# Last of sixteen experts added by a one-hot product instead of a scatter, with the other experts' sums reloaded beside it

## What is computed

```python
def expert_choice_ffn(h, w_router, w1, w3, w2):      # h: (B, L, D)
    cap = CAPACITY_FACTOR * L // N_EXPERTS           # 64 latent, 16 context tokens per expert
    aff = softmax(h @ w_router)
    gate, idx = lax.top_k(swapaxes(aff, 1, 2), cap)  # each expert chooses its tokens
    xs = h[idx]
    ye = (silu(xs @ w1) * (xs @ w3)) @ w2 * gate
    return zeros((L, D)).at[idx].add(ye)
...
x = x + g2 * expert_choice_ffn(h2, ...)
```

## Time and profile before

| | of the profiled execution |
|---|---|
| time, span | 3056.43 us, 3054.6 us |
| mean granted TensorE clock | 0.965 |
| PE busy | 2809.3 us (92%) |
| VectorE, ScalarE, GpSimd busy | 1882.3, 1501.3, 360.1 us |
| bytes moved by DMA | 595.31 MB |
| DMA rate while the experts run (page's slices) | 371 to 376 GB/s, most at 374 |
| cast of a 1 MB chunk, ScalarE | 1912 ns |
| low part of a chunk, VectorE | 2284 ns |
| load of 512 KB of w_in, issue to landing | 6.1 us (median of 72) |

### The profile page before, as it was taken

How to read it: one execution, slowest core, us unless ns; L and a number is a source line. 1 busy time by engine, 2 the same in 40 slices (tenths; PEclk the granted TensorE clock), 3 DMA queues, 4 the chain that set the end, 5 groups by cost and what they waited for, 6 DMA issues and landing times.

```text
span 3054.6 us, 40745 instructions
## 1 busy us (share of the span) xinstructions
PE 2809.3 (92%) x16674; PEld 2202.1 (72%) x16674; DVE 1882.3 (62%) x1929; ACT 1501.3 (49%) x1941; POOL 360.1 (12%) x233
## 2 busy tenths in 40 slices
PE   6999997999997999999879999989999599999996
PEld 5988876888875666666579777778889456666664
DVE  2166566652337888888633666658323578888884
ACT  4245454202127777777542455441122467777773
POOL 0411010000011101111113111100000211111110
PEclk8999999999998999999989999999999799999998
DMA  7132321221268999999822233122213399999995
GB/s 238 58 100 77 91 90 64 63 83 49 70 222 299 371 372 376 374 375 375 291 80 70 77 104 104 59 70 70 64 61 118 145 307 375 375 372 374 372 376 188
DMA packets 373482, 595.31 MB, mean 195 GB/s; under 512 B 12976, under 2 KB 164656, under 8 KB 373040
## 3 DMA queue, kind: packets, MB, share of 16 engines
q1 hardware_dynamic: 360208, 546.42, 51.0%
q0 software_dynamic: 13088, 46.28, 5.2%
HBM read 566.97 MB, written 25.69 MB: 194 GB/s over the span
## 4 chain that ended last, share of the span: by engine, by line
PE 70%; DMA 13%; DVE 7%; ACT 5%; issue 3%; SPq 1%; POOL 0%; DVEq 0%; POOLq 0%; ACTq 0%
PE ps L1270 17%; PE ps L1272 17%; PE ps L1271 17%; DMA m_raw<-in_w 9%; PE ps L1536 9%; DVE m_lo L1207 2%; PE ps L1461 2%; PE ps L1494 2%; DMA raw<-in_w_ada 1%; PE ps L1314 1%; ACT probs L520 1%; DVE stats L1020 1%; PE ps L1483 1%; DMA xg<-h_rows,token_of_slot 1%; SPq L314 1%
## 5 line engine op out<-in xcount | busy, mean ns | idle before, releaser
L798 ACT CAST m_hi<-m_raw 128x2048 fp32r<-128x2048 f32 x384 | 733.1, 1912 | 283.0 <-DMA m_raw<-in_w 264.4
L1207 DVE TENSOR_TENSOR m_lo<-m_raw,m_hi 128x2048 fp32r<-128x2048 f32 x384 | 861.5, 2284 | 14.3 <-PE ps L1272 13.2
L1270 PE MATMUL ps<-h_hi,w_hi 128*128 128x384 f32 (+2 forms) x1408 | 442.6, 314 | 17.1 <-DVE h_lo L943 9.4
L1272 PE MATMUL ps<-h_hi,w_lo 128*128 128x384 f32 (+2 forms) x1408 | 436.6, 310 | 0.0
L1271 PE MATMUL ps<-h_lo,w_hi 128*128 128x384 f32 (+2 forms) x1408 | 436.4, 310 | 0.0
L1270 PE MATMUL ps<-m_hi,xs_hi 128*80 128x512 f32 x1024 | 406.9, 397 | 3.4 <-DVE xs_lo L1224 3.4
L1271 PE MATMUL ps<-m_lo,xs_hi 128*80 128x512 f32 x1024 | 404.3, 395 | 0.0
L1272 PE MATMUL ps<-m_hi,xs_lo 128*80 128x512 f32 x1024 | 404.2, 395 | 0.0
L870 DVE TENSOR_TENSOR w_lo<-raw,w_hi 128x2048 fp32r<-128x2048 f32 x68 | 157.9, 2321 | 300.6 <-ACT w_hi L563 290.4
L563 ACT CAST w_hi<-raw 128x2048 fp32r<-128x2048 f32 x46 | 87.6, 1906 | 486.7 <-DMA raw<-in_w_gate 314.7
L1270 PE MATMUL ps<-w_hi,h_hi 128*128 128x256 f32 x960 | 284.4, 296 | 3.1 <-ACT pool_branch L647 1.8
(11 more groups left out here) (252 smaller groups left out, 4191.9 us busy)
## 6 DMA issues: line engine op xcount, KB each, us to landing
m_raw<-in_w SPq DMA_DIRECT2D x384, 1024.0 KB, 10.3
raw<-in_w_in SPq DMA_DIRECT2D x72, 512.0 KB, 6.1
raw<-in_w_ada SPq DMA_DIRECT2D x64, 512.0 KB, 4.7
raw<-in_w_gate SPq DMA_DIRECT2D x48, 512.0 KB, 6.7
ada_in_a<-in_w_ada SPq DMA_DIRECT2D x10, 1024.0 KB, 11.9
raw<-in_w_proj_a SPq DMA_DIRECT2D x16, 512.0 KB, 4.6
raw<-in_w_out SPq DMA_DIRECT2D x16, 512.0 KB, 6.0
moe_rows<-zeros POOLq DMA_DIRECT2D x10, 512.0 KB, 7.5
```

Source lines behind the costliest of these rows:

```text
L798: nc.scalar.copy(m_hi[:, g % HIS], m_raw[:, g % RAWS]).then_inc(s["m_high"], 1)
L1207: nc.vector.tensor_tensor(m_lo[:, g % LOS], m_raw[:, g % RAWS], m_hi[:, g % HIS].bitcast(F32), ALU.subtract).then_inc(s["msplit"], 1)
L1270: pe.matmul(out, wh, xh, start=first, stop=False, skip_group_check=True)
L1272: return pe.matmul(out, wl, xh, start=False, stop=last, skip_group_check=True)
```

## The change

The last expert is no longer scattered. Its result is split into `yh` and `yl` in SBUF (ScalarE and VectorE, one half of the channels at a time). A constant table with the token numbers 0 to 639 is loaded to 80 partitions (`places`), and VectorE compares it with each slot's token (`st[:, 62:63]`, a new copy at the routing), which gives the one-hot matrix `place` [80 slots, 640 tokens]. A product of `yh` and `yl` with `place` adds the rows at their tokens' columns, already transposed.

GpSimd loads `moe_rows`, which now holds the sums of the other 15 experts, as soon as expert 14's scatter has landed, beside the last expert's weights. `acc` becomes five tensors at places that are free then: two in slot 1 of `raw`, two behind `m_lo`, one in the value buffer. Because of the first two, SyncE's queue holds back layer 1's second load (slot 1) until all of TensorE's jobs are done.

TensorE's end is now 13 jobs. Jobs 0 to 4 transpose blocks 0 to 4 of `acc`, two after chunk 9 and three after chunk 10 of the last expert. Jobs 5 to 12 come after chunk 11, one for each block: a one-hot product for blocks 0 to 4, which VectorE adds to `x` in a second update; for blocks 5 to 7 the transposes are written as products with the identity and the one-hot product is added to them inside PSUM, with one update. The bank pairs are now 0, 2 and 6. The norm's sums move to banks 4 and 5. The split of the next layer's slot 0 comes after the last update on VectorE, that of slot 1 in the middle of the casts, as it does in layer 0.

```diff
+LAST_BANKS = (0, 2, 6)
+NTURN = 5
...
-        acc = sb("moe_tok", [P, TT, D], r_ring + 73728)
+        places = sb("token_numbers", [SLOTS, TOK], r_m)
+        place = sb("slot_of_token", [SLOTS, TOK], r_ring, F32R)
+        yh = sb("ye_hi", [SLOTS, D], r_ring + 4096, F32R)
+        yl = sb("ye_lo", [SLOTS, D], r_ring + 8192, F32R)
...
+        acc = [sb(f"moe_tok{t}", [P, D], at) for t, at in enumerate((r_raw + 8192, r_t2 + 32768, r_t2 + 36864, r_raw + 12288, r_v + 1280))]
...
@@ SyncE @@
                 for n, c0 in enumerate((POOL0, CONVB0, CONVA0)):
                     for u in range(2):
+                        if l and (n, u) == (0, 1):
+                            sp.wait_ge(s["acc_ps"], (NTURN + KT) * l)
                         wide(u, in_v[l, c0 // CW + u])
@@ GpSimd @@
                     pool.wait_ge(s["xs_ps"], seen("xs_ps"))
-                    if e < EXPERTS - 1:
-                        gather(e + 1)
+                    if e == EXPERTS - 1:
+                        pool.dma_start(places[:], places_in.partition_broadcast(SLOTS)).then_inc(s["places_in"], 16)
+                        break
+                    gather(e + 1)
...
-                    pool.dma_start(acc[:, t], moe_rows[t * P:(t + 1) * P, :]).then_inc(s["acc_in"], 16)
+                    pool.dma_start(acc[t][:], moe_rows[t * P:(t + 1) * P, :]).then_inc(s["acc_in"], 16)
@@ ScalarE @@
-                    if k == 3 and l == 0:
+                    if k == 3:
                         split_high(1, 1)
...
+                    if e == EXPERTS - 1:
+                        for c in range(2):
+                            act.wait_ge(s["mdone"], seen("mdone", 0) + e * NCH + 11 + c)
+                            nc.scalar.activation(yh[:, c * EW:(c + 1) * EW], ps[0:SLOTS, 4 + c, :], ACT.Copy, scale=gates[:, e:e + 1]).then_inc(s["ye_high"], 1)
+                        return
...
                 if l < DEPTH - 1:
                     split_high(0, 0)
-                    split_high(1, 1)
+                seen("x_new", NTURN)
@@ VectorE @@
-                if l == 0:
-                    split_low(1, 1)
+                split_low(1, 1)
...
+                nc.vector.tensor_copy(st[0:SLOTS, 62:63], ps[0:SLOTS, 7, EXPERTS - 1:EXPERTS])
...
+                        if (e, n) == (EXPERTS - 1, 10):
+                            dve.wait_ge(s["places_in"], seen("places_in", 16))
+                            nc.vector.tensor_scalar(place[:], places[:], st[0:SLOTS, 62:63], None, ALU.is_equal).then_inc(s["place_ready"], 1)
...
-                if l < DEPTH - 1:
-                    split_low(0, 0)
-                    split_low(1, 1)
-                for k in range(KT):
+                def ye_low(c):
+                    dve.wait_ge(s["ye_high"], seen("ye_high"))
+                    nc.vector.scalar_tensor_tensor(yl[:, c * EW:(c + 1) * EW], ps[0:SLOTS, 4 + c, :], gates[:, EXPERTS - 1:EXPERTS],
+                                                   yh[:, c * EW:(c + 1) * EW].bitcast(F32), ALU.mult, ALU.subtract).then_inc(s["ye_low"], 1)
+
+                for j in range(NTURN + KT):
+                    k = j if j < NTURN else j - NTURN
+                    if j == NTURN:
+                        ye_low(0)
+                    if j == NTURN + 2:
+                        ye_low(1)
+                    if NTURN <= j < 2 * NTURN:
+                        dve.wait_ge(s["x_new"], seen("x_new", 0) + k + 1)
                     dve.wait_ge(s["acc_ps"], seen("acc_ps"))
-                    b = 2 * (k % 3)
+                    b = LAST_BANKS[j % 3]
                     nc.vector.scalar_tensor_tensor(x[:, k, 0:LAT], ps[:, b, :], mods_of[l][:, 40 + k, 1:2], x[:, k, 0:LAT], ALU.mult, ALU.add)
...
+                if l < DEPTH - 1:
+                    split_low(0, 0)
@@ TensorE @@
+                def add_job(j):
+                    k, b = j if j < NTURN else j - NTURN, LAST_BANKS[j % 3]
+                    if j >= 3:
+                        pe.wait_ge(s["x_new"], seen("x_new", 0) + j - 2)
+                    if j == 0:
+                        pe.wait_ge(s["acc_in"], seen("acc_in", 16 * TT))
+                    both = j >= NTURN and k >= NTURN
+                    for t in range(TT if j < NTURN or both else 0):
+                        out, src = flat[:, b * 512 + t * P:b * 512 + (t + 1) * P], acc[t][:, k * P:(k + 1) * P]
+                        if both:
+                            pe.matmul(out, src, ident[:], start=t in (0, 4), stop=False, skip_group_check=True)
+                        else:
+                            ins = pe.transpose(out, src, ident[:])
+                    if j >= NTURN:
+                        if j == NTURN:
+                            pe.wait_ge(s["place_ready"], seen("place_ready"))
+                        if k % 4 == 0:
+                            pe.wait_ge(s["ye_low"], seen("ye_low"))
+                        for bank, a, e in ((b, 0, LAT), (b + 1, LAT, TOK)):
+                            pe.matmul(ps[:, bank, 0:e - a], yh[:, k * P:(k + 1) * P], place[:, a:e], start=not both, stop=False, skip_group_check=True)
+                            ins = pe.matmul(ps[:, bank, 0:e - a], yl[:, k * P:(k + 1) * P], place[:, a:e], start=False, stop=True, skip_group_check=True)
+                    ins.then_inc(s["acc_ps"], 1)
...
+                        if e == EXPERTS - 1 and n >= 9:
+                            for j in ((0, 1), (2, 3, 4), range(5, NTURN + KT))[n - 9]:
+                                add_job(j)
```

More of the change, by code:

```diff
@@ L271, in build @@
         mfull0 mfull1 mfull2 mfull3 mfull4 mfull5 m_high msplit mdone silu hidd hid_t ht_high ht_out xg_in xs_ps
-        xs_high xs_out ye_r scat acc_in acc_ps x_new m_ready out_ps out_sb y_out d_done
+        xs_high xs_out ye_r scat places_in place_ready ye_high ye_low acc_in acc_ps x_new m_ready out_ps out_sb y_out d_done
         dve act pool settled""".split()
@@ L876, in _, with sums_out @@
             spread4 = (ps[:, 6, :], ps[:, 7, 0:CTX])
-            def sums_out(sem):
+            def sums_out(sem, bank=6):
                 dve.wait_ge(s[sem], seen(sem))
-                nc.vector.tensor_copy(sums[:], flat[:, 6 * 512:6 * 512 + TOK]).then_inc(s["sums_out"], 1)
+                nc.vector.tensor_copy(sums[:], flat[:, bank * 512:bank * 512 + TOK]).then_inc(s["sums_out"], 1)
                 dve.wait_ge(s["sums_t"], seen("sums_t"))
@@ L899, in norm @@
             def norm(l):
-                sums_out("ss")
+                sums_out("ss", 4)
                 groups_sum(0, 4)
@@ L1339, in _, with group_sums @@
             cols = ((6, 0, LAT), (7, LAT, TOK))
-            def group_sums(src, first, last):
+            def group_sums(src, first, last, up=0):
                 for bank, a, b in cols:
                     for g in range(4):
-                        ins = pe.matmul(ps[32 * g:32 * g + 32, bank, 0:b - a], ones[:, 0:32], src(g, a, b), start=first, stop=last, skip_group_check=True)
+                        ins = pe.matmul(ps[32 * g:32 * g + 32, bank - up, 0:b - a], ones[:, 0:32], src(g, a, b), start=first, stop=last, skip_group_check=True)
                 return ins
@@ L1351, in squares_sums @@
                     pe.wait_ge(s["sq"], seen("sq", 4))
-                    ins = group_sums(lambda g, a, b: mm_[:, 4 * r + g, a:b], r == 0, r == 1)
+                    ins = group_sums(lambda g, a, b: mm_[:, 4 * r + g, a:b], r == 0, r == 1, 2)
                 ins.then_inc(s[sem], 1)
@@ L1696, in _ @@
                             turn_rows()
-                pe.wait_ge(s["ye_r"], seen("ye_r"))
-                pe.wait_ge(s["acc_in"], seen("acc_in", 16 * TT))
-                for k in range(KT):
-                    if k >= 3:
-                        pe.wait_ge(s["x_new"], seen("x_new", 0) + k - 2)
-                    b = 2 * (k % 3)
-                    for t in range(TT):
-                        ins = pe.transpose(flat[:, b * 512 + t * P:b * 512 + (t + 1) * P], acc[:, t, k * P:(k + 1) * P], ident[:])
-                    ins.then_inc(s["acc_ps"], 1)
-                seen("x_new", KT)
+                        if e == EXPERTS - 1 and n >= 9:
+                            for j in ((0, 1), (2, 3, 4), range(5, NTURN + KT))[n - 9]:
+                                add_job(j)
+                seen("x_new", NTURN + KT)
             pe.wait_ge(s["x_new"], seen("x_new", 0))
@@ L1769 @@
     small = np.concatenate([parts[n] for n in SMALL], axis=2)
-    ident, cos, sin, cnt = constants()
+    ident, cos, sin, cnt, places = constants()
     cvecs = np.stack([a["c_ctx"], a["c"][0]], 1).reshape(KT, P, 2).transpose(1, 0, 2)
@@ L1775 @@
         "w_proj_c": a["w_proj_c"], "w_gate": a["w_gate"], "w_out": a["w_out"], "w1": a["w1"], "w3": a["w3"], "w2": a["w2"],
-        "ident_in": ident, "cos_in": cos, "sin_in": sin, "inv_in": cnt,
+        "ident_in": ident, "cos_in": cos, "sin_in": sin, "inv_in": cnt, "places_in": places,
     }
```

8 lines of the change are left out of this document (4 added, 4 removed).

## The result

The changed kernel took 3040.91 us, the median of seven runs (3034.44 to 3043.95), against 3060.66 us before, seven runs on the same chip. The ratio is 0.9943, 95% interval 0.9932 to 0.9955: 17.4 us faster (0.0057 x 3060.66); the two medians differ by 19.8, of a forecast of 28.7 (3060.66 - 3032). The time lies in the forecast range and is 8.9 us above the point. The profiled execution took 3038.57 us.

What follows compares the result with a forecast made beforehand. PE is busy 92% of the span, so gains lie in its idle stretches at both layer ends. -15.6 + 0.7 - 12.0 + 0.2 = -26.7 us from 3056.43 gives 3029.7, placed at 3032 between two readings; range 3024 to 3044.

Steps and rivals of the forecast that it cites:

- The first rival: Last expert, both layers: loads start promptly, 1.3 us after issue, and delay chunk 10; PE loses 15.0 us, 3043.5; chance 0.15.
- my signs of being wrong: ScalarE idle several us on m_raw, TensorE idle on moe_tok, clock below 0.9 from chunk 9 to job 12, x waiting.
- Part 1: Loads beside the last expert's weights: first bytes 6.1 us after issue, little delay of chunk 10, some 4 us of chunk 11.
- Each us of delay of chunk 10 is one of PE: Last expert: TensorE waits for work behind chunk 10's cast, so its weights' delay passes to TensorE one for one.
- Delay of chunk 10: 0.3 us in layer 1: Last expert's weights: the loads delay chunk 10 by none in layer 0 and 0.3 us in layer 1.
- rival 2: Layer ends: waits or gaps put TensorE at half clock, 11.8 us lost in each layer, 3053; chance 0.05.
- Cost nothing: Chunk 11's weights, delayed some 4 us in both layers, cost no time because TensorE has two jobs in front.
- The landing: Loads of the sums land at 1509.6 to 1509.8 and 3012.0; job 0 waits 0.9 us in layer 0, none in layer 1.
- Part 2: Jobs 0 to 4 in front of chunks 10 and 11: 25 transposes add 3.85 us to PE before its last product.
- Part 3: Jobs 5 to 12 after the last product: last update 9.9 us behind it; gains 15.6 us and 12.0 us in the layers.
- Part 4: Work no longer hidden: layer 0's slot 0 split costs 0.7 us, at most 2.9; routing's copies nothing to 0.3.
- The sum: Whole kernel: -15.6 + 0.7 - 12.0 + 0.2 = -26.7 us.

Runs made afterwards that it cites:

- reload exposed: Changed kernel with no columns turned, all jobs last, and the reload issued only after the last product: 3061.52 us, ratio 1.0009 to the kernel before.
- held kernel: Changed kernel with loads issued after chunk 10's cast, jobs 0 to 4 after chunk 10, second `ye_low` earlier: 3039.52 us, ratio 0.993; again 3039.41 us.
- all in PSUM: Changed kernel with no block transposed ahead; all eight columns added inside PSUM after chunk 11: 3043.58 us, ratio 0.9952 to the kernel before.
- loads held: Changed kernel with GpSimd waiting for chunk 10's cast before it issues the loads, jobs left in place: 3045.72 us, ratio 0.9959 to the kernel before.
- doubled load: Changed kernel with a 2.62 MB memory-to-memory copy by GpSimd before the reload: 3056.78 us, ratio 0.9997 to the kernel before.

## Why the prediction was right, and where it was off

**The mechanism held.** Forecast and result agree in sign, place and most of the size: no wait for the sums after the last product, and of the 30 and 26 us between it and the last update 19 and 15 gone. The first rival (3043.5, chance 0.15) has its cause confirmed in part and lies nearer to the median than the forecast, so the result is between the two, where I had put 0.11. (The two aren't on one level: 3043.5 starts from the profiled execution, 3032 from a point above it.)

**Luck.** That the time fell inside the range owes something to luck. The range ends at 3044, and the changed kernel's second study gave 3045.39. In layer 0 two errors cancel. And of my signs of being wrong two showed in layer 1: ScalarE waited 3.09 us for chunk 10, 2.31 more than before, and the granted clock fell below 0.9 between chunk 9 and job 12.

**Part 1, when the loads start.** I took 6.1 us from issue to first bytes. The issue is at 2984.28. q0 had no packet in 2987 to 2988, and in 2988 to 2989 this (packets, MB, share of 16 engines):

```profile
q0 software_dynamic: 40, 0.18, 55.2%
q1 hardware_dynamic: 84, 0.17, 50.4%
```

So 3.7 to 4.7 us, between the 1.3 and the 6.1 that I weighed. The 6.1 was itself an upper bound: the four packets of the earlier trace rows lie in the second half of that microsecond, 5.6 to 6.1 us behind the issue. That the earlier trace rows were an indirect transfer, and this a direct one, was in the text (its issue is five times shorter) and should have moved the value. The Trainium skill, DMA: Bandwidth & Descriptors, Specifications, gives about 1 us for the first byte. Beside the weights no run here shows so little; with no weights moving the rows of before have 1.3 us, and in "reload exposed" the first packets move 1.3 us behind the issue, so there the trace agrees roughly. The sharing came as read from the earlier trace rows; in 2990 to 2991:

```profile
q0 software_dynamic: 66, 0.27, 68.4%
q1 hardware_dynamic: 66, 0.14, 35.7%
```

The Trainium skill, DMA: Bandwidth & Descriptors, Queues, rings and completion order, says that an engine takes its queues in turn, a packet each; the trace agrees, 66 against 66. Forecast for chunk 10: no delay, and 0.3 us. Measured: the cast's wait grew by 1.03 us in layer 0 (1.83 against 0.80) and by 2.31 in layer 1 (3.09 against 0.78, where chunk 9's cast had already waited 1.87 before the change). "Each us of delay of chunk 10 is one of PE" didn't hold in layer 0: of 1.03 us 0.37 became TensorE's idle, and T came 3.55 us later, below the 4.75 that I had. In layer 1 TensorE idled 2.43 us in the last expert (0.42 and 2.01) where it had idled 0.81 before, and then came something that I had priced only for longer stops, the half clock:

```profile
2994.99 0.46 PE L1301 MATMUL ps<-m_hi,hid_t_hi 128*80 128x512 f32 x1 [0.42 <-DVE hid_t_lo L1232]
...
2999.98 0.49 PE L1708 MATMUL ps<-ident,hid 80*128 80x80 f32 x4 [2.01 <-DVE hid L1227]
```

The one pause there before the change:

```profile
3009.18 0.50 PE L1677 MATMUL ps<-ident,hid 80*128 80x80 f32 x4 [0.81 <-DVE hid L1213]
```

The window behind the pause of 2.01 us:

```profile
3000.00:3004.50 4.50, 4.50 (x16) 2.81 (x17) 3.03 (x3) 1.76 (x2) 0.00 (x0) 0.65 0.01 4
```

The 0.65 is a mean of a part at 2.4 GHz and one at 1.2: seven of chunk 9's products went at 0.43 and not 0.23 us, and the chunk took 4.28 us against 2.83 in layer 0, 1.5 more. The step that failed is "Delay of chunk 10: 0.3 us in layer 1", with rival 2's "against" ("the fall stood behind some 12 us of idle, and here the gaps are below 1"). The held kernel takes just these away and has 3.4 to 3.9 us of layer 1 back. What decides between a pause of 2.01 us in two profiles and one of 0.82 or 1.23 in two others with the same code up to there is open.

Chunk 11 was delayed more than forecast too: its cast started 22.9 and 24.7 us behind the scatter's issue, where the forecast had it landed at 21.3 and 22.1. "Cost nothing" held thanks to the two jobs in front, with nothing to spare in layer 0; without them ("all in PSUM") TensorE waited 1.0 to 1.1 us.

**The landing.** Forecast 1509.6 to 1509.8, with a wait of 0.9 us in layer 0. There was none in either layer; jobs 0 and 1 followed chunk 9 at once. For `moe_tok` the trace has, in layer 1:

```profile
DMA to landing us min/median/max: 7.2/9.7/12.8
```

The fifth was issued at 2987.0, so all were there by 2999.8, which is 25.0 us behind expert 14's scatter (2974.81), 4.7 us before job 0. The forecast had 26.1 (3012.0 - 2985.86). An earlier start and more sharing came out close to a late start and less of it, which is luck.

**Part 2.** 25 transposes at 0.154 us were to cost 3.85. In the chain above 15 take 1.64, 0.109 each, and all 25 take 2.7 to 2.9: in a long row each costs less than in the group of five that I took the earlier trace rows.

**Part 3, after T.** Forecast 9.9 us, measured 11.03 in layer 0 (1514.34 to 1525.37) and 11.04 in layer 1 (3013.10 to 3024.14). The one-hot jobs were right: 0.30 + 0.23 + 0.06 + 0.13 = 0.72 against 0.76, and the first job with both parts starts its products with the identity at T + 4.4 (forecast 4.3). The mis-sized term is those products. I priced them like transposes, five in 0.77; they take 1.17 us. Each one is two records in the trace, of 0.117:

```profile
L1722 PE MATMUL ps<-ident,moe_tok x60: 275/275/377, 1518.7 to 3022.2; 128*128 128x128 f32 x60
...
L1724 PE MATMUL ps<-ident,moe_tok x50: 270/272/388, 1505.6 to 3010.1; 128*128 128x128 f32 x50
```

The first line is 30 instructions in the code (five for each of three jobs in two layers), the second 50 transposes with a record each. A full float32 product of 128 columns is 0.235 us; one of F32R operands at 128 columns is 0.06 where it isn't the last. The Trainium skill, FP8 and Floating Point Precision, TensorE Precision Notes, has true FP32 as four passes through the array; the trace agrees, 0.235 against 0.06. The job is 1.80 us, not 1.53: three of them are 0.8 of the 1.1 us.

**Part 4.** From the last update to layer 1's rotation tables it takes 0.9 us longer, forecast 0.7 with 0.2 for the routing's copies, which the stages don't show. The chain has the reason that was given: `split_low`, 2.21 us behind the last update, and then the sums' rows.

**The sum.** Forecast 26.7 us at the profile's own level. Measured in the ends: 15.7 - 0.9 + 8.9 = 23.7. In layer 0 the two errors cancel, by luck: T came 1.2 us sooner than forecast (cheap transposes, no wait for the sums), the last update 1.1 us later behind it. In layer 1 they add: T 2.0 us late (6.15 and not 4.2 behind the old one: 1.6 more idle time and 1.5 for the clock, of which 0.3 was foreseen, less 1.0 for the transposes, and 0.2 that I can't place), and the same 1.1 behind it. The runs show 17.4 and then 12.2 us by the ratios, 19.8 and 13.8 by the medians. The difference to 23.7 is not at the ends. A part stands behind the last update: 11.6 to 12.7 us in all six profiles of kernels with five turned columns, 10.5 to 11.3 in the four of the kernel before and of those with none. In those six, 1.8 to 2.2 us pass between the last bytes moved and the end of the span, in the other four 0.8. These are 1 to 2 us that the forecast didn't have, and the runs don't show why it is there. The rest lies in stages that vary by up to 8 us for one and the same kernel; more than that isn't shown.

## What to carry over

A load that is moved beside a stream of weights isn't free when it is issued early: it takes its share packet by packet, and the larger packets take more bytes (here 0.27 against 0.14 MB in 1 us). Place it by the last stream item that is on the path (issue it once that one has landed), and put its first use as late as the order of the work allows. The first without the second gave nothing here ("loads held"); the second without the first wasn't run. And to add float32 data inside PSUM with a product with the identity took TensorE 1.17 us for a column against 0.55 for its transposes, but it spares the element engine an update: with no column turned layer 0's end was 3.5 us longer than with five, with all eight 1.0 to 1.3.

## What the runs showed of the hardware that was not expected

- A pause of TensorE of 2.01 us was followed by a granted clock of 0.65 and 0.64 over the next 4.5 us in the two profiles of the changed kernel, and one of 2.62 us with the loads held by 0.72 over 6 us, while one of 2.23 us in its other layer left it at 1.00. Behind pauses of 0.37 to 1.47 us ahead of chunk 9 it was 1.00 each time; behind 3.94 and 6.56 us ("doubled load") it was 0.62 and 0.65 over 4.5 us. A pause of 2 us can already cost the clock, and need not.
- The stretch from the last update to the end was 10.5 and 11.3 us before the change and 12.7 and 11.6 after it, though the output's code is the same. In the six profiles of kernels with five turned columns the last microseconds are quiet for 1.8 to 2.2 us, and each has one packet in the queue `q8 instruction` in the last 11 us; the six others have 0.8 us and no such packet. Whether the packet is the cause isn't shown.
- The first 100 us of layer 1's mixing stage ran at a granted clock of 1.00 in one execution of a kernel and of 0.95 in the next.
